# Decoder layer in fp32 on Trainium2: the feed-forward products as seven block products in two passes

## What is computed

```python
def ffn_sublayer(x, w_up, w_down, g_pre, g_post):      # w_up (2048, 8192), w_down (8192, 2048)
    h = rmsnorm(x, g_pre)
    a = jnp.square(jax.nn.relu(jnp.einsum('ntd,df->ntf', h, w_up)))
    return x + rmsnorm(jnp.einsum('ntf,fd->ntd', a, w_down), g_post)
```

## Time and profile before

| | |
|---|---|
| median of 3 runs | 2207.6 us (2205.54 to 2207.78) |
| span of the profiled execution | 2207.5 us |
| that execution's own time beside it | about 0.1 us more, as the median |
| up to the first feed-forward matmul | 592.3 us |
| from 654.40 to 2164.90 us | TensorE without a stop |
| bytes moved | 192.7 MB, 87 GB/s on average |

### The profile page before, as it was taken

One profiled execution on the slowest core, in us unless ns is written; L12 is line 12 of the kernel. 1 busy time (PEld: TensorE's weight loads), 2 busy tenths in 40 slices (PEclk: granted clock), 3 DMA queues, 4 the chain that ended last, 5 costly groups with the idle time before them and its releaser, 6 DMA issues.

```text
span 2207.5 us, 39376 instructions
## 1 busy us (share of the span) xinstructions
PE 2151.8 (97%) x16878; PEld 2123.3 (96%) x16878; DVE 966.5 (44%) x1212; ACT 533.8 (24%) x743; POOL 149.3 (7%) x135
## 2 busy tenths in 40 slices
PE   7999999999889999999999999999999999999996
PEld 7999989999889999999999999999999999999995
DVE  3455436322574344343434444343344434334446
ACT  5244414222231212121121212112121112212132
POOL 0000023100350000000000000000000000000024
PEclk9999989999889999999999999999999999999996
DMA  5421112522112222222223222222222222222222
GB/s 174 148 64 52 58 58 67 180 86 86 57 48 86 87 90 91 86 86 86 86 85 95 86 86 86 88 90 85 88 86 86 88 93 86 86 86 86 86 67 81
DMA packets 181548, 192.70 MB, mean 87 GB/s; under 512 B 6080, under 2 KB 177480, under 8 KB 180911
## 3 DMA queue, kind: packets, MB, share of 16 engines
q1 hardware_dynamic: 178016, 181.96, 26.2%
q10 hardware_dynamic: 3479, 9.99, 1.2%
HBM read 186.95 MB, written 7.37 MB: 88 GB/s over the span
## 4 chain that ended last, share of the span: by engine, by line
PE 94%; DVE 4%; DMA 0%; issue 0%; ACT 0%; SPq 0%; POOL 0%; DVEq 0%; ACTq 0%; POOLq 0%
PE banks L1271 89%; PE banks L1416 1%; DVE acts_lo L1138 1%; DVE x1T L1213 1%; PE banks L1237 1%; PE banks L1386 1%; DVE x1T L1143 1%; PE banks L1404 1%; DVE w_lo L808 1%; DMA x_tok<-in_x_sample 0%; PE banks L1458 0%; PE banks L1245 0%; PE banks L1457 0%; DVE k_twice L871 0%; DVE x1T L1147 0%
## 5 line engine op out<-in xcount | busy, mean ns | idle before, releaser
L808 DVE TENSOR_TENSOR w_lo<-w_raw,w_hi 128x1024 fp32r<-128x1024 f32 x330 | 421.4, 1277 | 688.6 <-ACT w_hi L545 685.0
L1271 PE MATMUL banks<-acts_hi,w_hi 128*128 128x272 f32 x3232 | 681.2, 292 | 17.3 <-DVE acts_lo L1138 5.3
L1271 PE MATMUL banks<-acts_hi,w_lo 128*128 128x272 f32 x3232 | 674.2, 290 | 0.0
L1271 PE MATMUL banks<-acts_lo,w_hi 128*128 128x272 f32 x3232 | 671.9, 290 | 0.0
L545 ACT ACTIVATE w_hi<-w_raw 128x1024 fp32r<-128x1024 f32 x330 | 349.3, 1059 | 1305.6 <-PE banks L1271 1298.6
L1271 PEld LDWEIGHTS banks<-acts_hi,w_hi 128*128 128x128 f32 x3232 | 512.9, 190 | 24.9 <-issue 14.8
L1271 PEld LDWEIGHTS banks<-acts_lo,w_hi 128*128 128x128 f32 x3232 | 513.6, 191 | 0.0
L1271 PEld LDWEIGHTS banks<-acts_hi,w_lo 128*128 128x128 f32 x3232 | 510.2, 191 | 0.0
L1271 PE MATMUL banks<-mlp_lo,w_hi 128*128 128x272 f32 x2048 | 424.8, 288 | 0.0
L1271 PE MATMUL banks<-mlp_hi,w_hi 128*128 128x272 f32 x2048 | 422.5, 287 | 0.0
L1271 PE MATMUL banks<-mlp_hi,w_lo 128*128 128x272 f32 x2048 | 422.3, 287 | 0.0
(11 more groups left out here) (187 smaller groups left out, 732.6 us busy)
## 6 DMA issues: line engine op xcount, KB each, us to landing
w_raw<-in_w_up SPq DMA_DIRECT2D x128, 512.0 KB, 3.6
w_raw<-in_w_down SPq DMA_DIRECT2D x128, 512.0 KB, 3.3
w_raw<-in_w_in SPq DMA_DIRECT2D x40, 512.0 KB, 3.6
w_raw<-in_w_out SPq DMA_DIRECT2D x32, 512.0 KB, 3.4
x_tok<-in_x_prompt SPq DMA_DIRECT2D x8, 512.0 KB, 9.1
x_tok<-in_x_prompt ACTq DMA_DIRECT2D x4, 1024.0 KB, 8.0
out<-w_raw SPq DMA_DIRECT2D x16, 256.0 KB, 2.6
old_k<-in_cache_k ACTq DMA_DIRECT2D x1, 1024.0 KB, 19.5
```

The costliest lines, as they stand in the source:

```text
L808: nc.vector.tensor_tensor(w_lo[:, k % SPLIT_SLOTS, :], w_raw[:, k % RAW_SLOTS, :], w_hi[:, k % SPLIT_SLOTS, :].bitcast(F32), ALU.subtract) ...
L1271: ins = nc.tensor.matmul(out[:, h, :], w, x[:, h * H:(h + 1) * H], start=first, stop=last)
```

## The change

The up projection becomes 32 groups (`UP_GROUPS`) of 256 output columns, the down projection 64 groups (8 chunks of 1024 hidden features, 8 pairs of output tiles). In a group all blocks are taken by twos: even and odd tile of the contraction, first and second output tile, first and second half of the tokens. Instead of eight block products there are seven (`NP`), on sums of blocks. The weight sums of a group (`t1` to `t4`) are made by GpSimd, the activation sums of the up pass once by VectorE (`h_sum`), those of the down pass by GpSimd (`activation_sums`) behind each up group. The seven products gather in PSUM in part (`STARTS`, `BANK`) and VectorE adds them to `quads` or `y_sum` (`take`). Every weight block or sum is rounded by ScalarE into `splits` in SBUF (`high_part`), and the rest is taken by VectorE from there (`low_part`).

The up pass ends before the down pass begins. The hidden activations, rounded and rest, go to HBM (`mlp_kept`, 1.95 MB per up group) and come back in seven parts per chunk (`load_part`). x1 goes to HBM too and is read back for the end. The activations are scaled by their token's norm and by `g_ffn` ahead of the products (`scale_tiles`), so no product starts before the norm's scales. SBUF is laid out by fixed offsets, and all loops of these stages and of the output projection are straight code. The diff, cut to its core:

```diff
+    NP = 7
+    UP_GROUPS = F // UNIT_N
+    UP_J = KT // 2
+    DOWN_J = 4
+    CHUNK = DOWN_J * UNIT_N
+    CHUNKS = F // CHUNK
+    DOWN_GROUPS = CHUNKS * OUT_PAIRS
+    N_UP = NP * UP_GROUPS
+    CHUNK_N = NP * OUT_PAIRS
+    N_ALL = N_UP + NP * DOWN_GROUPS
...
+        BANK = (None, 3, None, 2, None, 2, None)
+        GOES_TO = (0, 0, 1, 3, 3, 1, 2)
+        FRESH = (True, False, True, True, False, False, True)
+        STARTS = (True, True, False, True, False, False, False)
+        KEPT_AT = (2, 0, 3, 4, 5, 6, 1)
+        QUAD_AT = (3, 1, 0, 2)
+        T_NEEDS = {2: 3, 3: 1, 4: 2, 6: 4}
+        def bank_of(G, i):
+            return G % 2 if BANK[i] is None else BANK[i]
...
+        def split_free(N):
+            if N < N_UP:
+                return N - 2 if N >= 3 else 0
+            d = N - N_UP
+            return N_UP + d - 3 if d >= 4 else N_UP - 2 + d // 2
...
+            def blocks_split(G):
+                sp.wait_ge(part_hi, NP * G + 6)
+                sp.wait_ge(part_lo, NP * G + 6)
+                sp.wait_ge(t_ready, 4 * G + 4)
+            def store_hi(g):
+                sp.wait_ge(mlp_rounded, g + 1)
+                sp.dma_start(mlp_kept[g, :, :, 0, :], mlp_hi[:].bitcast(F32)).then_inc(hi_stored, 16)
+            def store_lo(g):
+                sp.wait_ge(mlp_rest, g + 1)
+                sp.dma_start(mlp_kept[g, :, :, 1, :], mlp_sums[:]).then_inc(lo_stored, 16)
+            def load_part(c, i):
+                sp.dma_start(mlp_parts[:, c % 2, i].bitcast(F32),
+                             mlp_kept[c * DOWN_J:(c + 1) * DOWN_J, :, KEPT_AT[i]].rearrange("j p h n -> p j h n")
+                             ).then_inc(mlp_landed[i], 16)
...
+            sp.wait_ge(hp_lo, 5)
+            load_up(1)
+            for g in range(UP_GROUPS):
+                if g > 0:
+                    store_hi(g - 1)
+                    store_lo(g - 1)
+                if g < UP_GROUPS - 2:
+                    blocks_split(g)
+                    load_up(g + 2)
...
+            def t1(G):
+                if G > 0:
+                    gp.wait_ge(part_hi, NP * (G - 1) + 4)
+                    gp.wait_ge(part_lo, NP * (G - 1) + 4)
+                blocks_landed(G)
+                nc.gpsimd.tensor_tensor(t_of(G, t_x), block_of(G, 0, 1), block_of(G, 0, 0), ALU.subtract).then_inc(t_ready, 1)
+            def t3(G):
+                if G > 0:
+                    gp.wait_ge(part_hi, NP * (G - 1) + 5)
+                    gp.wait_ge(part_lo, NP * (G - 1) + 5)
+                nc.gpsimd.tensor_tensor(t_of(G, t_z), block_of(G, 1, 1), block_of(G, 0, 1), ALU.subtract).then_inc(t_ready, 1)
+            def t2(G):
+                if G > 0:
+                    gp.wait_ge(part_hi, NP * G)
+                    gp.wait_ge(part_lo, NP * G)
+                gp.wait_ge(t_ready, 4 * G + 1)
+                nc.gpsimd.tensor_tensor(t_of(G, t_y), block_of(G, 1, 1), t_of(G, t_x), ALU.subtract).then_inc(t_ready, 1)
+            def t4(G):
+                gp.wait_ge(part_hi, NP * G + 3)
+                gp.wait_ge(part_lo, NP * G + 3)
+                gp.wait_ge(t_ready, 4 * G + 3)
+                nc.gpsimd.tensor_tensor(t_of(G, t_y), block_of(G, 1, 0), t_of(G, t_y), ALU.subtract).then_inc(t_ready, 1)
+            def activation_sums(g):
+                gp.wait_ge(squared, 2 * g + 2)
+                a12, a22, a11, s2, s1, s3, s4 = [mlp_sums[:, i, :] for i in range(NP)]
+                a21 = quads[:, QUAD_AT[2], :]
+                nc.gpsimd.tensor_tensor(s1, a21, a22, ALU.add).then_inc(a_summed, 1)
+                nc.gpsimd.tensor_tensor(s3, a11, a21, ALU.subtract).then_inc(a_summed, 1)
+                gp.wait_ge(a_summed, 4 * g + 1)
+                nc.gpsimd.tensor_tensor(s2, s1, a11, ALU.subtract).then_inc(a_summed, 1)
+                gp.wait_ge(a_summed, 4 * g + 3)
+                nc.gpsimd.tensor_tensor(s4, a12, s2, ALU.subtract).then_inc(a_summed, 1)
...
+            for G in range(ALL_G):
+                t4(G)
+                if 0 < G <= UP_GROUPS:
+                    activation_sums(G - 1)
+                if G + 1 < ALL_G:
+                    t1(G + 1)
+                    t3(G + 1)
+                    t2(G + 1)
...
+            def high_part(N):
+                source_ready(N)
+                if split_free(N):
+                    act.wait_ge(product_done, split_free(N))
+                nc.scalar.activation(split_of(N, 0), weight_of(N), ACT.Copy).then_inc(part_hi, 1)
...
+            def mlp_high(g):
+                act.wait_ge(a_summed, 4 * g + 4)
+                if g > 0:
+                    act.wait_ge(hi_stored, 16 * g)
+                nc.scalar.activation(mlp_hi[:], mlp_sums[:], ACT.Copy).then_inc(mlp_rounded, 1)
...
+            for N in range(4, N_ALL):
+                high_part(N)
+                G, i = divmod(N, NP)
+                if i == 4 and 0 < G < UP_GROUPS:
+                    mlp_high(G - 1)
...
-            def second_low(kt):
-                dve.wait_ge(h_hi, KT + kt + 1)
-                nc.vector.scalar_tensor_tensor(out=acts_lo[:, kt, :], in0=x1T[:, kt, :], scalar=g_ffn[:, kt:kt + 1],
-                                               in1=acts_hi[:, kt, :].bitcast(F32), op0=ALU.mult, op1=ALU.subtract).then_inc(h_lo, 1)
...
+            def low_part(N):
+                dve.wait_ge(part_hi, N + 1)
+                if split_free(N):
+                    dve.wait_ge(product_done, split_free(N))
+                nc.vector.tensor_tensor(split_of(N, 1), weight_of(N),
+                                        split_of(N, 0).bitcast(F32), ALU.subtract).then_inc(part_lo, 1)
+            def take(N):
+                G, i = divmod(N, NP)
+                dve.wait_ge(product_done, N + 1)
...
+                if fresh:
+                    nc.vector.tensor_copy(dst, src).then_inc(taken, 1)
+                else:
+                    dve.wait_ge(taken, N)
+                    nc.vector.tensor_tensor(dst, dst, src, ALU.add).then_inc(taken, 1)
+            def square_relu(g):
+                dve.wait_ge(taken, NP * (g + 1))
+                if g > 0:
+                    dve.wait_ge(lo_stored, 16 * g)
+                nc.vector.scalar_tensor_tensor(out=mlp_sums[:, 0:3, :], in0=quads[:, 1:4, :], scalar=0.0, in1=quads[:, 1:4, :],
+                                               op0=ALU.max, op1=ALU.mult).then_inc(squared, 1)
...
+            def mlp_low(g):
+                dve.wait_ge(mlp_rounded, g + 1)
+                nc.vector.tensor_tensor(mlp_sums[:], mlp_sums[:], mlp_hi[:].bitcast(F32), ALU.subtract).then_inc(mlp_rest, 1)
...
+            def scale_tiles(t):
+                for j in range(UP_J):
+                    kt = 2 * j + t
+                    dve.wait_ge(x1_moved[kt // 4], 16)
+                    ins = nc.vector.scalar_tensor_tensor(out=x1T[:, kt, :], in0=x1T[:, kt, :], scalar=g_ffn[:, kt:kt + 1],
+                                                         in1=norm_scale[:], op0=ALU.mult, op1=ALU.mult)
+                ins.then_inc(h_scaled, 1)
+                dve.wait_ge(h_scaled, t + 1)
...
+            scale_tiles(0)
+            h_sum(s3, a11, a21, ALU.subtract)
+            h_low(0, a11, 1)
+            scale_tiles(1)
+            h_low(1, a12, 3)
+            h_sum(s1, a21, a22, ALU.add)
+            dve.wait_ge(h_summed, 2)
+            h_sum(s2, s1, a11, ALU.subtract)
+            dve.wait_ge(h_summed, 3)
+            h_sum(s4, a12, s2, ALU.subtract)
+            h_low(2, s2, 5)
...
+            for N in range(3, N_UP):
+                take(N)
+                if N < N_UP - 3:
+                    low_part(N + 3)
+                elif N < N_UP - 1:
+                    low_part(N_UP + 2 * (N - (N_UP - 3)))
+                    low_part(N_UP + 2 * (N - (N_UP - 3)) + 1)
+                G, i = divmod(N, NP)
+                if i == 2 and G > 0:
+                    mlp_low(G - 1)
+                if i == 6:
+                    square_relu(G)
...
+            H_READY = (1, 2, 3, 4, 6, 7, 7)
+            def taken_before(G, i):
...
+                last_group = NP * (G - 1)
+                return (last_group, last_group + 2, NP * G + 1, last_group + 6, NP * G + 3, NP * G + 4, NP * G + 5)[i]
+            def strassen_product(N):
...
+                pe.wait_ge(part_hi, N + 1)
+                pe.wait_ge(part_lo, N + 1)
+                if taken_before(G, i) > 0:
+                    pe.wait_ge(taken, taken_before(G, i))
+                if G == 0:
+                    pe.wait_ge(hp_lo, H_READY[i])
...
+                for j in range(pairs):
+                    if G < UP_GROUPS:
+                        xh, xl = h_parts[i][0][:, j, :], h_parts[i][1][:, j, :]
+                    else:
+                        c = (G - UP_GROUPS) // OUT_PAIRS
+                        xh, xl = mlp_parts[:, c % 2, i, j, 0, :], mlp_parts[:, c % 2, i, j, 1, :]
+                    wh, wl = split_of(N, 0)[:, j, :], split_of(N, 1)[:, j, :]
+                    first = STARTS[i] and j == 0
```

(49 more changed lines are left out.)

561 lines of the change are left out of this document (319 added, 242 removed).

## The result

The changed kernel takes 2306.15 us in the median of four runs (2305.56 to 2308.44), the one before beside it 2207.69. The ratio is 1.0449 (95% interval 1.0435 to 1.0464): slower by 4.5%, where 193 us of TensorE's work were taken out. The span of the profiled execution is 2303.8 us.

A forecast was written before the change was run, and what follows sets the result against it. VectorE's and GpSimd's two-SBUF-input operations, excluding each other, plus queue waits were taken to bound the up stage. Sum: 627 + 66 + 31 x 27.7 + 706 + 2.5 + 41 = 2301 us; range 2140 to 2355.

The forecast's parts named there:

- Up groups: Up stage: 26.1 us per group plus 1.6 us for the lower clock, 27.7 us, for 31 groups.
- The walk: One up group followed operation by operation through its loop of waits: 26.1 us, before the clock's loss.
- Down groups: Down stage: 56 groups of 10.9 us and the last eight of 12.0 us, together 706 us.
- the bounds given: Down group: TensorE's 10.53 us and VectorE's queue of 11.8 us.
- Transfers costed at nothing: Both stages: transfers at 190 GB/s at most add nothing; without cover, seven loads before the down stage late first, some 25 us.
- Ahead of the first product: From the turn of the squares at 627 us to the end of group 0: 66 us.
- the door's sum: VectorE's and GpSimd's two-SBUF-input operations added as if run singly: 35.8 us before the turn, 24.3 us per up group.
- Tail: Kernel's end: 41.0 us from the turn to the span's end, plus 2.5 us for the last tile.
- The first (clock stays up): Up stage: stops broken up, none over 2 us, so 31 x 1.6 us less: 2251 us; chance 0.17.
- The second (sums at 1.8 ns per element): GpSimd's new sums run faster: up group 23.4 us, total 2141, or 2191 if the clock falls too; chance 0.25.
- The third (no exclusion): VectorE and GpSimd don't hold each other up for these shapes; TensorE remains the bound: 2056 us, chance 0.08.
- The fourth: TensorE's 0.1254 us step grows with 24 matmuls in a row to one bank, or loads late: above 2355; chance 0.08.

The follow-up runs named there:

- the filler run: Changed kernel plus 24 matmuls with unread results ahead of product 5's waits in up groups 1 to 30: 2265.89 us, ratio 1.0261.
- The runs in which the exclusion costs nearly nothing: Changed kernel with GpSimd memsets for weight sums, 2072.72 us; changed kernel with rests from PSUM, `mlp_low` moved later and activation sums ahead of `t4`, 2075.65 us.
- the last version: Changed kernel with rests from PSUM copies, `mlp_low` behind the taking of product 3 and activation sums ahead of `t4`: 2075.65 us, ratio 0.9403.
- the run with activation sums first: Changed kernel with GpSimd's activation sums of the group before made ahead of the last weight sum (`t4`): 2258.96 us, ratio 1.0239.
- the run with both orders: Changed kernel with `mlp_low` behind the taking of product 3 and activation sums ahead of `t4`, rests still from SBUF: 2229.65 us, ratio 1.01.

## Why the prediction came out

Forecast 2301, measured span 2303.8: the sign, the mechanism and the size. Term by term:

- **Up groups: right.** The walk gave 26.1 and the clock 1.6; measured are 25.7 (the filler run) and 1.5. Its items match the turn shown above: sums 5.1 (5.1), roundings 2.7 (2.8), the held rest 3.4 (3.0), `mlp_low` 2.06 (2.1), tile 0.5 (0.5), products 5 and 6 at the lower clock 7.6 (7.7), rounding and rest 2.4 (2.4), squarings 3.9 (3.6). Two sizes were off: a weight sum of 1024 takes 2.40 us for 2.54, so the waits for it are shorter, and the stop is 3.5 us for 4.3. Two of the groups in the trace, those without the lower clock, took 25.7 us, most 27.2, and the last is shorter. From the end of product 6 of group 0 (688.8) to that of group 31 (1528.7) are 840 us; the forecast had 859.
- **Down groups: some 17 us too low.** A group takes 11.15 us for 10.9, and one of the last eight 12.4 for 12.0. The first lies between the bounds given, the second above the one count given for it. A rest of a raw block beside a sum lasts 1.7 us for its own 0.68; one stop of 0.35 is left per group, and two of 0.7 in each of the last eight. That is 14 + 3 us.
- **Transfers costed at nothing: wrong by some 8 us at one place.** The prediction named the seven loads ahead of the down stage as what would be late first. They were late. VectorE's timeline, SyncE's queue and TensorE's timeline in the kernel after:
```profile
1519.75 2.13 DVE L1443 TENSOR_TENSOR mlp_sums<-mlp_sums,mlp_hi 128x1904 f32<-128x1904 f32 x1
```
```profile
1521.91 0.52 SPq L524 DMA_DIRECT2D mlp_kept<-mlp_sums  x1
1522.75 12.28 SPq L527 DMA_DIRECT2D mlp_parts<-mlp_kept  x7
```
```profile
1530.36 0.36 PE L1944 MATMUL banks<-mlp_parts,splits 128*128 128x272 f32 x1 [1.70 <-DMA mlp_parts<-mlp_kept]
1533.22 0.36 PE L1944 MATMUL banks<-mlp_parts,splits 128*128 128x272 f32 x1 [1.12 <-DMA mlp_parts<-mlp_kept]
...
1548.61 0.57 PE L1944 MATMUL banks<-mlp_parts,splits 128*128 128x272 f32 x1 [2.20 <-DMA mlp_parts<-mlp_kept]
```
  Seven products each wait for their part, 9.5 us in all. From 1533 to 1540 the transfers move 389 GB/s at a share of 1.06: once asked for, they come fast. The average rate per group (190 GB/s) said nothing of this. At the turn from one stage to the other, no part of the first chunk can come before the up stage's activations leave their place, and product 0 of the last up group, which frees the place of the first two parts, ended at 1507.8. But the loads stand in SyncE's queue behind two stores, and the second of these waits for `mlp_low`, until 1521.9. So the first load was issued some 15 us later than its place was free. That these stores are the whole of the lateness isn't shown: no run has another order in this queue. The down stage takes 731.5 us with it, for 706.
- **Ahead of the first product: 4 us too high, with misses of both signs.** The turn of the squares starts at 622.1 us (627 forecast). GpSimd works through its 23 operations from 587.82 to 622.03 without a wait, 34.2 us, where the door's sum was 35.8. That sum, from 588.3 on, ended at 624.1; the 2.9 us from there to the 627 are worked out nowhere in the prediction. The scales are there 11.7 us after the turn, not 7.8. VectorE's timeline in the kernel after:
```profile
622.28 6.42 DVE L1408 TENSOR_TENSOR splits<-raw_up,splits 128x1024 fp32r<-128x1024 f32 x2 [3.68 <-ACT splits L996]
...
628.62 0.15 DVE L1082 COPY ss<-banks 128x4 f32<-128x4 f32 x1
...
633.04 0.72 DVE L1450 COPY norm_scale<-banks 128x544 f32<-128x544 f32 x1 [2.73 <-PE banks L1563]
```
  Two rests of group 0, each held up by a weight sum, stand in VectorE's queue ahead of the copy of the turned sums, which TensorE had ready at 625.9. The forecast put them behind. In the version with rests from PSUM TensorE waits 2.06 us for the root, for 4.41 here. Group 0 ends 66.7 us after the turn (66 forecast), so what follows the scales is some 3 us shorter than forecast.
- **Tail: right.** 43.6 us from the last product to the end, for 43.5.
- In sum: -4.9 + 0.7 - 18.8 + 25.5 + 0.1 = +2.6 us on the forecast's 2301.2. That the total came so close is chance: misses of 19 and 26 us have opposite signs.

**The rivals.** The first (clock stays up) didn't hold: the clock fell in all but two of groups 2 to 30. It was priced at 1.6 us per group, and fillers give 1.5 back, 40 us of the 50. The second (sums at 1.8 ns per element) falls with 2.40 us per 1024, 2.34 ns. My 2.45 was an average of the earlier trace rows without a fixed part: 2.40, 1.29 and 0.77 us for 1024, 512 and 272 lie on a line of 0.18 us and 2.17 ns per element. The Trainium skill (GPSIMD Engine Reference, 3.1) gives 4497 ns for 2048, and that line, carried on to a size that no run here has, gives 4.6 us. The third (no exclusion) had 2056 us; it falls with the rests of 3.1 us beside sums. The runs in which the exclusion costs nearly nothing give 2072.7 and 2075.7. The fourth falls: TensorE's step is 0.1261 us in the up stage of the last version (21.19 by 168) and 0.1256 in its down stage (10.55 by 84), though 24 matmuls in a row add to one bank.

**What was taken from too little.** The prediction saw the exclusion in one place and in one pattern that repeats, and held it for a sum of two-input operations. That was enough for the size, but the part that costs is the queue order on top: the excluding work of 24.3 us leaves the group 27.2 long, 1.5 of them the clock's, and one place in a queue is worth 2.6.

## What to carry to other kernels

Before work is moved to GpSimd, count what both engines read twice from SBUF: VectorE's operations with two SBUF inputs and GpSimd's sums from SBUF ran one after the other here, and where their sum passes TensorE's time they are the bound though each engine looks half idle. A copy of one operand in PSUM, written by an engine with room, frees them; here it was worth 188 us of 2306. Where a short stage follows a long one, cost the transfers at the turn by themselves and not by the stage's average, and look at what stands in the queue behind each operation that can be held up.

## What the runs showed of the hardware

- A memset of 1024 on GpSimd (0.96 us) and a VectorE operation with two SBUF inputs run side by side; a sum (2.4 us) and the same operation don't. Which of the two waits is settled by who is issued first: a rest issued 0.14 us after a sum waits it out (3.3 us), a sum issued after a squaring of 816 waits too (3.04 us).
- A squaring whose two inputs are the same SBUF tile is held up as well (2.64 us for 0.43).
- The granted clock falls near the end of a stop, at no fixed distance from it. Behind the stop that ended at 1226.72 TensorE starts at full pace, and its matmuls slow down from 1227.6 on, for 3.4 us. In groups 2 to 30 the kernel after has 29 long stops (28 of 3.5 us, one of 3.0). Behind 27 of them stands such a stretch at the lower level, which begins between 0.15 us before the restart and 1.5 us after it; behind two, which end at 983.6 and 1389.8, there is none.
- In the run that moves `mlp_low` the stops of 1.44 us, one per group from 733 us on, left the clock at 1.00. In the run with activation sums first every stop of 4.48 us from 787 us on is followed by the lower level and none of the 1.90. TensorE's windows in that run, first behind a stop of 4.48 us, then behind one of 1.90 (columns as in the earlier trace rows):
```profile
1043.78:1049.78 6.00, 6.00 (x36) 0.72 0.87 250
1068.60:1074.60 6.00, 5.93 (x45) 1.00 0.87 249
```
  In the run with both orders 10 of the 29 stops of 2.0 to 2.3 us are followed by it, and 19 are not. So the length of the last stop alone doesn't decide it there.
- GpSimd's sum costs 0.18 us and 2.17 ns per element in these shapes; the 1.35 us for 544 in the earlier trace rows lies on that line (1.36), the 5.36 for 2176 with a rounded result above it (4.90).
- The transfer engines moved 389 GB/s over 7 us at the turn of the stages, and 424 over 7 us from 412.3 in the same kernel; the 349 over 4 us of the earlier trace rows wasn't the most that they can do.
